# The first four k-tiles of both output projections issued beside the last attention steps, with fewer PSUM banks for the C heads

## What is computed

```python
y = jnp.concatenate([ya, yb, yn], axis=-1) @ w_out[l]      # 4 A heads, 6 B heads, 6 C heads, 64 columns each
if l < DEPTH - 1:                                          # layer 0 only: 256 context tokens as well
    ctx = ctx + gt_c * (jnp.concatenate([ya_c, yb_c, yn_c], axis=-1) @ w_out[l])
x = x + gt[:, None] * y
```

## Time and profile before

| what | us |
|---|---|
| median of 3 runs (lowest, highest) | 1282.99 (1276.28, 1285.08) |
| the profiled execution: its own time | 1282.64 |
| its span, first to last instruction | 1280.9 |
| PE busy in the span | 1150.2 (90%) |
| DVE, ACT, POOL busy | 726.2, 602.4, 250.8 |

### The profile page before, as it was taken

One profiled execution on the slowest core, in us unless ns is written; L12 is line 12 of the kernel. 1 busy time (PEld: TensorE's weight loads), 2 busy tenths in 40 slices (PEclk: granted clock), 3 DMA queues, 4 the chain that ended last, 5 costly groups with the idle time before them and its releaser, 6 DMA issues.

```text
span 1280.9 us, 16699 instructions
## 1 busy us (share of the span) xinstructions
PE 1150.2 (90%) x5877; PEld 915.1 (71%) x5877; DVE 726.2 (57%) x1322; ACT 602.4 (47%) x1174; POOL 250.8 (20%) x324
## 2 busy tenths in 40 slices
PE   5977799898978987899989898998889999999987
PEld 2655578676666765688767686887678887888875
DVE  3466776786661744554544666554465555565543
ACT  3433353444761443454563553443444445544553
POOL 1482330363004112202300203000021211121100
PEclk8998899898998988999989999998899999999999
DMA  9656344424012323222202674553446665444301
GB/s 334 134 163 188 92 135 132 131 84 118 32 48 58 115 68 100 63 67 82 72 29 66 234 216 146 165 182 130 148 149 182 184 185 156 132 123 121 120 1 49
DMA packets 79001, 157.92 MB, mean 123 GB/s; under 512 B 5760, under 2 KB 6056, under 8 KB 78664
## 3 DMA queue, kind: packets, MB, share of 16 engines
q1 hardware_dynamic: 75592, 147.41, 36.8%
q0 software_dynamic: 3328, 9.46, 3.4%
HBM read 153.73 MB, written 3.11 MB: 122 GB/s over the span
## 4 chain that ended last, share of the span: by engine, by line
PE 71%; DVE 11%; ACT 7%; POOL 5%; issue 4%; DMA 2%; SPq 0%; ACTq 0%; POOLq 0%; DVEq 0%
PE bank L707 17%; PE bank L709 16%; PE bank L708 16%; PE bank L848 5%; PE bank L833 3%; PE bank L823 3%; POOL small L1415 2%; DVE w_lo L1605 2%; PE bank L923 2%; ACT w_hi L1019 2%; DVE work L1625 2%; PE bank L896 2%; PE bank L908 1%; PE bank L727 1%; POOL stage L490 1%
## 5 line engine op out<-in xcount | busy, mean ns | idle before, releaser
L707 PE MATMUL bank<-w_lo,h_hi 128*128 128x512 f32 (+1 forms) x1152 | 464.2, 403 | 28.0 <-DVE h_lo L1674 10.6
L709 PE MATMUL bank<-w_hi,h_hi 128*128 128x512 f32 (+1 forms) x1152 | 449.7, 390 | 0.0
L708 PE MATMUL bank<-w_hi,h_lo 128*128 128x512 f32 (+1 forms) x1152 | 449.3, 390 | 0.0
L1605 DVE TENSOR_TENSOR w_lo<-raw,w_hi 128x1024 fp32r<-128x1024 f32 x224 | 285.6, 1281 | 280.4 <-ACT w_hi L1019 279.1
L1019 ACT ACTIVATE w_hi<-raw 128x1024 fp32r<-128x1024 f32 x224 | 235.9, 1057 | 295.6 <-PE bank L709 250.1
L707 PEld LDWEIGHTS bank<-w_lo,h_hi 128*128 128x128 f32 x1152 | 224.2, 195 | 80.1 <-issue 31.4
L709 PEld LDWEIGHTS bank<-w_hi,h_hi 128*128 128x128 f32 x1152 | 223.0, 194 | 45.4
L708 PEld LDWEIGHTS bank<-w_hi,h_lo 128*128 128x128 f32 x1152 | 224.2, 195 | 40.4 <-issue 0.2
L848 PE MATMUL bank<-work,stage 128*128 128x128 f32 x640 | 95.1, 291 | 1.8 <-ACT stage L1206 1.6
L1197 ACT ACTIVATE stage<-bank,small 128x512 f32<-128x512 f32 (+1 forms) x96 | 57.0, 596 | 71.7 <-DVE small L1821 71.5
L848 PEld LDWEIGHTS bank<-work,stage 128*128 128x128 f32 x640 | 85.7, 205 | 3.4 <-ACT stage L1206 2.8
(11 more groups left out here) (172 smaller groups left out, 1097.3 us busy)
## 6 DMA issues: line engine op xcount, KB each, us to landing
raw<-in_b_w_in_dram SPq DMA_DIRECT2D x80, 512.0 KB, 3.7
raw<-in_w_in_dram SPq DMA_DIRECT2D x56, 512.0 KB, 3.8
raw<-in_a_w_in_dram SPq DMA_DIRECT2D x48, 512.0 KB, 4.2
raw<-in_w_ada_dram SPq DMA_DIRECT2D x32, 512.0 KB, 3.8
work<-in_w_ada_dram SPq DMA_DIRECT2D x16, 512.0 KB, 11.4
raw<-in_w_out_dram SPq DMA_DIRECT2D x16, 512.0 KB, 3.5
raw<-in_a_w_out_dram SPq DMA_DIRECT2D x16, 512.0 KB, 4.4
raw<-in_b_w_out_dram SPq DMA_DIRECT2D x8, 512.0 KB, 3.6
```

The lines of the kernel that those rows point to most:

```text
L707: pe.matmul(bank, hT(h_hi, ph, kt, tt), w_lo[:, s, k, lo:lo + w], start=first, stop=False)
L708: pe.matmul(bank, hT(h_lo, ph, kt, tt), w_hi[:, s, k, lo:lo + w], start=False, stop=False)
L709: mm = pe.matmul(bank, hT(h_hi, ph, kt, tt), w_hi[:, s, k, lo:lo + w], start=False, stop=last)
L1605: dve.tensor_tensor(w_lo[:, i % SPLIT, :, :], raw[:, PIECE_AT[p] % RAW, :, :], w_hi[:, i % SPLIT, :, :].bitcast(F32), ALU.subtract).then_i ...
```

## The change

- `AHEAD` lists sixteen products (blocks) per layer, each a call of `product` (three matmuls of 512 columns). Layer 0: chunk 0, k-tiles 0 to 3, four tiles. Layer 1: both chunks, k-tiles 0 to 3, two tiles. They are issued by PE at the very start of steps 46 to 61 (one a step, layer 0) and 25 to 32 (two a step, layer 1), and are left out of the output projection. Their accumulators are banks 0 to 3.
- From step 46 (layer 0) or 25 (layer 1) the C heads have two score banks (4, 5), one for turned probabilities (6), one for outputs (7).
- The four `split` tasks move to steps 40 to 43 in layer 0 and 19 to 22 in layer 1.
- The pieces of `out1` come in the order chunk 0 pairs 0 and 1, chunk 1 pairs 0 and 1, chunk 0 pairs 2 and 3, chunk 1 pairs 2 and 3. What is left of `out1` is one loop over tiles with both chunks in it; ACT and DVE first split the last four pieces, then DVE scales and adds both chunks of a tile and ACT squares both halves.

```diff
--- before.py
+++ after.py
@@ -98,8 +98,18 @@
 
 
 
+AHEAD = {"out0": [(("out0", 0, pair), k, tt) for tt in ALL_TILES for pair in (0, 1) for k in (0, 1)],
+         "out1": [(("out1", c, pair), k, tt) for tt in X_TILES for c in (0, 1) for pair in (0, 1) for k in (0, 1)]}
+AHEAD_FROM = {"out0": 46, "out1": 25}
+
+
+def out1_pieces():
+
+    return [("out1", c, pair) for first in (0, 2) for c in (0, 1) for pair in (first, first + 1)]
+
+
 PIECES = (first_pieces() + ada_pieces(1, (4, 5)) + pieces_of("out0") + pieces_of("in1")
-          + pieces_of("out1") + pieces_of("gin") + pieces_of("gout") + pieces_of("din") + pieces_of("dout"))
+          + out1_pieces() + pieces_of("gin") + pieces_of("gout") + pieces_of("din") + pieces_of("dout"))
 PIECE_AT = {p: n for n, p in enumerate(PIECES)}
 
 SPLITS = [p for p in PIECES if not p[0].startswith("ada")]
@@ -188,8 +198,11 @@
     tts = ALL_TILES if layer == 0 else X_TILES
     for i, tt in enumerate(tts):
         tasks.setdefault(first + i, []).append(("y", tt))
+    ph = f"out{layer}"
     for i in range(SPLIT):
-        tasks.setdefault(len(units_of(layer)) - SPLIT + i, []).append(("split", i))
+        tasks.setdefault(AHEAD_FROM[ph] - 2 - SPLIT + i, []).append(("split", i))
+    for n, block in enumerate(AHEAD[ph]):
+        tasks.setdefault(AHEAD_FROM[ph] + n // (1 + layer), []).append(("block", *block))
     return tasks
 
 
@@ -712,6 +725,15 @@
                 elif k == 1 and tt == tiles_of(ph)[-1]:
                     mm.then_inc(*piece_used.at(p))
 
+            def ahead(p, k, tt):
+
+                ph, c, pair = p
+                if (p, k, tt) == AHEAD[ph][0]:
+                    ring[0] = 0
+                if tt == 0 and k == 0:
+                    weights(p)
+                product(ph, c, p, k, tt)
+
             def weights(p):
                 pe.wait_ge(*weights_hi.seen(p))
                 pe.wait_ge(*weights_lo.seen(p))
@@ -732,6 +754,12 @@
                 pairs = PROJ[ph][1] // 2
                 for c in range(PROJ[ph][0]):
                     pieces = [(ph, c, pair) for pair in range(pairs)]
+                    if ph == "out0" and c == 0:
+                        pieces = pieces[2:]
+                    if ph == "out1":
+                        pieces = out1_pieces()[4:]
+                        if c == 0:
+                            continue
                     if c == 0 and ph == "in0":
                         first_chunk(pieces)
                         continue
@@ -776,7 +804,7 @@
                             if tt == tts[-1] and p == ending[-1] and FOLLOWING[ph]:
                                 norm_turns(FOLLOWING[ph], 1 if tt == 3 else 0)
                             for k in range(2):
-                                product(ph, c, p, k, tt)
+                                product(ph, p[1], p, k, tt)
                     if between:
                         between(c)
 
@@ -798,6 +826,7 @@
                 solo = len(steps_beside(f"in{layer}"))
                 ph = f"in{layer}"
                 fill = fill_of(layer)
+                shared = range(solo, AHEAD_FROM[f"out{layer}"])
                 s_use = [0]
 
                 def score(u, i):
@@ -811,7 +840,7 @@
                     for m in range(2 if kind == "A" else 1):
                         n = s_use[0]
                         s_use[0] += 1
-                        ring = SCORE_BANKS if i < solo else SCORE_BANKS + (2, 3)
+                        ring = SCORE_BANKS + (2, 3) if i in shared else SCORE_BANKS
                         bank = take(pe, ring[n % len(ring)], "score", layer, n)
                         if kind == "A":
                             col = (2 * h + m) * 32
@@ -827,7 +856,7 @@
                 def turn(i):
                     u = units[i]
                     pe.wait_ge(*(weighed.seen(u) if u[2] == "A" else exps.seen((layer, prob_at[(u, 0)]))))
-                    bank = take(pe, TURN_BANK if i + 1 < solo or i % 2 else 0, "pT", u)
+                    bank = take(pe, 0 if i + 1 in shared and i % 2 == 0 else TURN_BANK, "pT", u)
                     kt0 = 0 if u[1] in X_TILES else 2
                     for j in range(kt0, 4):
                         mm = pe.transpose(bank[:, j * P:(j + 1) * P], probs[prob_slot(layer, u, 0)][:, j * P:(j + 1) * P], ident[:, :])
@@ -841,7 +870,7 @@
                         for tt in ALL_TILES:
                             pe.wait_ge(*values_kept.seen((ph, c, tt)))
                     pe.wait_ge(*pT_a.seen(u))
-                    bank = take(pe, OUT_BANK if i + 2 < solo or i % 2 else 1, "out", u)
+                    bank = take(pe, 1 if i + 2 in shared and i % 2 == 0 else OUT_BANK, "out", u)
                     vcol, _ = value_columns(kind, h)
                     kt0 = 0 if qt in X_TILES else 2
                     for j in range(kt0, 4):
@@ -850,6 +879,9 @@
                     mm.then_inc(*attended.at(u))
 
                 def step(i):
+                    for task in fill.get(i, ()):
+                        if task[0] == "block":
+                            ahead(*task[1:])
                     if i == 0:
                         score(units[0], 0)
                     for n in scored_at(units, i):
@@ -1289,15 +1321,18 @@
                 for tt in tiles_of(ph):
                     y_part(ph, tt, 1)
                 following = FOLLOWING[ph]
-                project(ph, lambda ph, c: None)
-                for tt in tiles_of(following):
-                    act.wait_ge(*added.seen((ph, 0, tt)))
-                    square(following, tt, 0)
+                if layer == 0:
+                    project(ph, lambda ph, c: None)
+                    for tt in tiles_of(following):
+                        act.wait_ge(*added.seen((ph, 0, tt)))
+                        square(following, tt, 0)
+                else:
+                    split_until(SPLIT_AT[(ph, 1, 3)] + 1)
 
                 def last_squares(tt):
-                    if tt in tiles_of(following):
-                        act.wait_ge(*added.seen((ph, 1, tt)))
-                        square(following, tt, 1)
+                    for half in range(layer == 0, 2):
+                        act.wait_ge(*added.seen((ph, half, tt)))
+                        square(following, tt, half)
 
                 end_of(ph, lambda tt: None, last_squares)
                 if layer == 0:
@@ -1786,10 +1821,11 @@
                 u = (ph, c, tt)
                 who = 2 if ph == "out1" else 0 if tt in X_TILES else 1
                 dve.wait_ge(*projected.seen(u))
-                dve.tensor_tensor(out_part[tt % 2], bank_of("proj", *u)[:, :], ada_gate[:, who, c * NC:(c + 1) * NC], ALU.mult) \
+                part = out_part[(c if ph == "out1" else tt) % 2]
+                dve.tensor_tensor(part, bank_of("proj", *u)[:, :], ada_gate[:, who, c * NC:(c + 1) * NC], ALU.mult) \
                     .then_inc(*out_scaled.at(u))
                 dve.wait_ge(*out_scaled.seen(u))
-                dve.tensor_tensor(x[:, tt, c * NC:(c + 1) * NC], x[:, tt, c * NC:(c + 1) * NC], out_part[tt % 2], ALU.add) \
+                dve.tensor_tensor(x[:, tt, c * NC:(c + 1) * NC], x[:, tt, c * NC:(c + 1) * NC], part, ALU.add) \
                     .then_inc(*added.at(u))
 
             def process_out(ph, c):
@@ -1971,8 +2007,13 @@
             project_with("in1", process_in, attention1(1))
             for tt in X_TILES:
                 y_part("out1", tt, 1)
-            project("out1", process_out)
-            end_of("out1", out_tile)
+            split_until(SPLIT_AT[("out1", 1, 3)] + 1)
+
+            def both_chunks(ph, c, tt):
+                out_tile(ph, 0, tt)
+                out_tile(ph, 1, tt)
+
+            end_of("out1", both_chunks)
 
             def process_gin(ph, c):
                 if c < 4:
```

## The result

| | before | after |
|---|---|---|
| median of 11 runs each, us | 1283.34 | 1288.39 |
| lowest to highest, us | 1276.28 to 1285.23 | 1287.03 to 1290.87 |
| ratio, 95% interval | | 1.0045 [1.0033, 1.0058] |
| profiled execution: own time / span, us | 1282.64 / 1280.9 | 1290.87 / 1289.1 |
| mean granted clock | 0.949 | 0.943 |

The change costs 5 us of the median (1288.39 - 1283.34), by the interval 4.2 to 7.4 us. Forecast was +7.4 us, 1290.0. The sign and the size hold; within 1% it is "the same".

The account below looks back on a forecast made before the run. The prediction took PE to bound the kernel, busy 90% of the span and throughout most tail steps. Layer 0 at +3.1 and layer 1 at +4.3 gave +7.4, from 1282.6 to 1290.0 us; range 1277 to 1299.

Parts of the forecast that it names:

- Blocks at their full price: Steps with blocks, both layers: PE has no room, 0.68 us a block; +9.3 in layer 0, +10.9 in layer 1.
- The rival by which nothing is gained since blocks only change places: Both layers: 21.8 us in and out, no late start of out1; sum +3.1, 1285.7 us; shares a chance of 0.10.
- Fewer banks, 0: Both tails: products ahead of the scores give exponentials time, so no cost; 0.4 us at the end of layer 1.
- The ring, +9.8: Layer 0, steps 40 to 43: exponentials, w_hi, w_lo and next maximum run one after another, 4.15 us a step; +9.8 us.
- The clock, +2: Layer 0, stretched steps 40 to 43: PE thinly busy, granted clock may fall, costing 0 to 5 us; +2 taken.
- the first three blocks, +0.5: Layer 0, steps 46 to 48: products stand by waits for bank 6, so nearly free; 0.5 us for all three.
- Turned halves, -0.8: Layer 0, behind the attention: they start at full clock after a denser end; -0.8 of 8.4 us, between 0 and -2.
- Out0, -10.9 - 0.3: Layer 0 output projection: 48 products' matmuls less, -10.9 us; second chunk no longer waits for a slot, -0.3.
- Out1: Layer 1 output projection: products start 3.2 us late, gin starts 8.3 us earlier; -7.0 us in all, bounds -10.9 and -5.
- The ring absent: Rival, layer 0, steps 40 to 43: splits fit into slack, 9.8 + 2.0 fall away, 1278.2 us; chance 0.22.
- The clock rival: Layer 0: clock stays low through steps 44 to 50, and second scores wait for banks; 1297 us; chance 0.18.
- Out1 helped more: Rival, layer 1 output projection: late start is hidden and all 10.9 us come back; 1286 us; chance 0.10.

Follow-up runs that it names:

- the run with the ring opened: The changed kernel with DVE's half of each split task one step later, behind the next unit's maximum: 1282.91 us, ratio 1.0004 to the kernel before.

## Why the prediction was right, and where it was off

- *Blocks at their full price.* Right: 0.70 us each in both layers (0.68 forecast), PE busy 27.01 of 27.90 us beside them. The rival by which nothing is gained since blocks only change places shares this part; it fell on out1's late start.
- *Fewer banks, 0.* Right for the steps with blocks, and by a margin that matters: alone they cost 8.7 us. By the median that is also more than the forecast's bounds for the scores allowed (5.4 + 1.8 = 7.2 us). What the term left out is the very end of layer 0, where units without a block follow each other on single banks. Timeline of PE of the kernel after, the last attend and the first turned half:

```profile
399.44 0.68 PE L877 MATMUL bank<-work,stage 128*128 128x128 f32 x4 [0.47 <-DVE work L1892]
...
400.59 0.63 PE L702 MATMUL bank<-ident,work 128*128 128x128 f32 x4 [0.47 <-DVE work L1892]
```

  Each attend waits for the output ahead of it (0.25 us, then 0.47 here, on DVE line 1892). From the turn of unit 61 to the first turned half it takes 400.59 - 395.64 = 4.95 us against 9.77, so -4.8 where -6.0 was forecast. That is the term mis-sized.
- *The ring, +9.8.* Right to 0.1 us, period and sum; the run with the split tasks alone shows the ring, and the run with the ring opened shows that 5.3 us of the whole hang on it. That this is less than 9.9 has two reasons, both seen there: opened, four steps still take 2.37 us each, so that only 7.5 come back at unit 45, and 2.5 of these are lost by the turn of unit 47, 0.9 with the longer wait for bank 6 and 1.6 to a fall of the clock.
- *The clock, +2, and the first three blocks, +0.5.* The fall came, to 0.50 from 348 to 356. From the maximum of unit 45 to the scores of step 49 the lag grows by 11.8 - 9.9 = 1.9 us, where both terms together were 2.5.
- *Turned halves, -0.8.* Measured -0.5 (7.87 against 8.33 us). They are thin by themselves and lose the clock again.
- *Out0, -10.9 - 0.3.* From its first product to in1's second tile 15.1 - 3.2 = 12.0 us are saved, 0.8 more than forecast. The errors of layer 0 (1.2, 0.3, -0.6, -0.8) cancel to +3.2 against +3.1, so that the sum fits to 0.1 us is luck, though each term lies near.
- *Out1.* First product late by 15.44 - 11.79 = 3.65 us more than the turned half (forecast 3.2); DVE's scaling of chunk 1, tile 0, starts 7.3 us earlier after the first turned half (8.3). So layer 1 is +5.7 in this execution where +4.3 was forecast. The chain itself, three `w_lo`, then `gin`, is the one named. (The forecast says 1.4 us for the second scaling and adds 1.3.)
- *Rivals.* The ring absent fell by the 4.16 us. The clock rival had its fall, but it ended before step 46 (the block at 358.06 runs at full clock), not in step 50, and the banks hardly bound, so it did not decide. Out1 helped more fell with the 2.94 us wait.

The size: the forecast's terms sum to +7.4, the profiled execution shows +8.6 at `gin` and +6.8 at its end, the medians say +5.0. The runs of each layer alone (+1.2 and +3.0 us) are both below the terms of their layer, by one or two us each; in layer 0 the interval (to +2.8) just excludes the term, in layer 1 (to +4.7) it does not. I do not know which term is smaller in the median run than in the profiled one.

## What to carry to other kernels

Before moving work beside a stretch, look at whether the engine that it needs is idle there, and who ends its idle time: products put into a stretch where PE is busy throughout cost their full time, and the same products (in layer 1 half of them) in the waits between turned halves gained 1.3%. When two in-order engines each get half of a task, and their other work depends on each other, the place of the halves matters more than their length: put the second half behind the next thing that the other engine waits for. And when work is moved away, ask what it covered where it stood; here it had hidden the preparation of the next weights.

## What was not expected of the hardware

- Filling the 8.4 us of the turned halves changed the granted clock from 0.50 to 0.81 there and from 0.51 to 1.00 behind, and gained 8.0 us in layer 0 up to in1's second tile, where the filled gap alone was 8.40 - 4.11 = 4.3 us of PE time. This thin stretch was paid for twice, in itself and in the dense one behind it.
- One and the same set of instructions on ACT and DVE took 4.16 or 2.37 us a step by order alone. Each time the clock fell somewhere: from 348 to 356 in the closed ring, and around 354 to 356 in the opened one.
- Two score banks in place of four, and single ones for turned probabilities and outputs, cost next to nothing with 0.70 us of other matmuls ahead of the scores (1.23 us for a pair against 1.13), and 0.7% of the whole time without.
